# Routing stage of a two-layer mixture-of-experts backbone: expert matrices requested at the end of the output products, the prompt tile's stores on ScalarE's queue, two matrices behind the gathers, the affinities turned inside the last product

## The reference, cut to what matters

```python
def ec_moe(x, router_w, w_gate, w_up, w_down):
    bsz, n_tok, _ = x.shape
    cap = n_tok * EC_CAPACITY // N_EXPERTS
    aff = jax.nn.softmax(jnp.einsum('btd,de->bte', x, router_w).astype(jnp.float32), axis=-1)
    gate, idx = lax.top_k(jnp.swapaxes(aff, 1, 2), cap)
    bidx = jnp.arange(bsz)[:, None, None]
    xe = x[bidx, idx]
    hid = jax.nn.silu(jnp.einsum('becd,edf->becf', xe, w_gate)) * jnp.einsum('becd,edf->becf', xe, w_up)
    ye = jnp.einsum('becf,efd->becd', hid, w_down) * gate[..., None].astype(x.dtype)
    return jnp.zeros_like(x).at[bidx, idx].add(ye)
```

## Time and profile before

| What | us |
|---|---|
| three runs | 1542.63, 1538.18, 1542.36 |
| median | 1542.36 |
| profiled execution, its own time | 1539.78 |
| its span, first to last instruction | 1538.0 |
| TensorE busy in the span | 1337.5 (87%) |
| DMA engines, mean rate over the span | 220 GB/s |

### The profile page before, as it was taken

One profiled execution on the slowest core, in us unless ns is written; L12 is line 12 of the kernel. 1 busy time (PEld: TensorE's weight loads), 2 busy tenths in 40 slices (PEclk: granted clock), 3 DMA queues, 4 the chain that ended last, 5 costly groups with the idle time before them and its releaser, 6 DMA issues. The chain is left out here.

```text
span 1538.0 us, 17799 instructions
## 1 busy us (share of the span) xinstructions
PE 1337.5 (87%) x6717; PEld 933.7 (61%) x6717; DVE 1007.3 (65%) x1355; ACT 805.0 (52%) x1126; POOL 438.0 (28%) x264
## 2 busy tenths in 40 slices
PE   5989999677792999999989999988697499999995
PEld 1756567454681666666658877555376366666663
DVE  1536415765646888888866338566554688888875
ACT  3612116533422777777755277544322377777772
POOL 0002007554002044444330032355101024444430
PEclk7999999798995999999989999999798599999997
DMA  9578840300517999999951120040231999999954
GB/s 366 224 287 315 325 156 8 150 29 28 218 72 275 348 360 382 381 381 379 368 159 19 59 59 5 8 198 1 92 151 60 372 343 383 380 376 376 379 179 170
DMA packets 63598, 339.11 MB, mean 220 GB/s; under 512 B 16724, under 2 KB 21464, under 8 KB 45080
## 3 DMA queue, kind: packets, MB, share of 16 engines
q1 hardware_dynamic: 57464, 317.31, 54.1%
q0 software_dynamic: 6048, 20.65, 5.7%
HBM read 314.04 MB, written 23.89 MB: 220 GB/s over the span
## 5 line engine op out<-in xcount | busy, mean ns | idle before, releaser
L1696 POOL TENSOR_TENSOR modrow<-modrow,proj 80x1024 f32<-80x1024 f32 x30 | 132.6, 4420 | 311.2 <-ACT modrow L1814 311.2
L1846 DVE TENSOR_TENSOR wlow<-wraw,proj_rounded 128x2048 fp32r<-128x2048 f32 x96 | 217.0, 2288 | 5.3 <-ACT proj_rounded L1788 5.3
L1725 PE MATMUL psum<-wlow,proj_rounded 128*80 128x512 f32 x512 | 202.7, 396 | 0.0
L1788 ACT ACTIVATE proj_rounded<-wraw 128x2048 fp32r<-128x2048 f32 x96 | 180.0, 1909 | 9.2 <-PEq L1377 9.2
L1724 PE MATMUL psum<-proj_rounded 128*80 128x512 f32 x376 | 151.3, 402 | 2.1 <-DVE proj_rounded L1851 2.1
L1726 PE MATMUL psum<-proj_rounded 128*80 128x512 f32 x376 | 148.2, 394 | 0.0
L1304 POOL TENSOR_SCALAR ring<-ring,small 128x640 f32<-128x640 f32 x64 | 99.7, 1563 | 109.1 <-DVE small L1261 108.6
L1287 ACT ACTIVATE ring<-psum,small 128x640 f32<-128x640 f32 (+1 forms) x80 | 56.7, 709 | 100.1 <-DVE small L1255 100.1
L1846 DVE TENSOR_TENSOR wlow<-wraw,xr_rounded 128x2048 fp32r<-128x2048 f32 x32 | 73.3, 2291 | 43.7 <-ACT xr_rounded L1788 43.7
L1725 PEld LDWEIGHTS psum<-wlow,proj_rounded 128*80 128x80 f32 x512 | 76.8, 150 | 39.8 <-issue 1.2
L1725 PE MATMUL psum<-wlow,small_rounded 128*80 128x512 f32 x256 | 100.8, 394 | 0.0
(11 more groups left out here) (469 smaller groups left out, 3251.2 us busy)
## 6 DMA issues: line engine op xcount, KB each, us to landing
wraw<-in_exp_w_gate_dram SPq DMA_DIRECT2D x32, 2048.0 KB, 13.2
wraw<-in_exp_w_up_dram SPq DMA_DIRECT2D x32, 2048.0 KB, 12.6
wraw<-in_exp_w_down_dram SPq DMA_DIRECT2D x32, 2048.0 KB, 13.9
ring<-in_ada_w_dram SPq DMA_DIRECT2D x29, 1024.0 KB, 6.5
hold<-in_ada_w_dram SPq DMA_DIRECT2D x14, 1024.0 KB, 6.4
ring<-in_ev_w_in_dram SPq DMA_DIRECT2D x4, 2048.0 KB, 11.9
xr<-x_rows SPq DMA_DIRECT2D x15, 512.0 KB, 6.9
ring<-in_od_w_in_dram SPq DMA_DIRECT2D x3, 2048.0 KB, 17.0
```

Source lines behind the costliest of these rows:

```text
L1696: pool.tensor_tensor(ye[0:CAP, :], ye[0:CAP, :], g2[0:CAP, :], ALU.mult).then_inc(s["ye"], 1)
L1725: pe.matmul(dst, xs[:, 0, k, :], wl, start=False, stop=False)
L1788: act.activation(high_of(m, h), raw_of(m, h), ACT.Copy).then_inc(s["high"], 1)
L1846: dve.tensor_tensor(low_of(m, h), raw_of(m, h), high_of(m, h), ALU.subtract).then_inc(s["low"], 1)
```

## The change

In the out block SyncE stores only the four sample tiles. It then waits for the ten half products and requests matrices 2 to 5. The prompt tile's two stores are issued by ScalarE: x behind the root, xm behind a wait for the normalised tile, both ahead of the prompt tile's turned copy. The last half product is cut after two of its eight k steps, and the sample's affinities are turned there. VectorE takes four rounds of the sample ahead of the prompt tile's scaling and four behind it. In the experts block SyncE waits for gathers 0 and 1 to land before it requests matrices 6 and 7, and all that stands behind them in its queue waits too.

```diff
-                    for t in range(TILES):
+                    for t in range(ST):
                         sp.wait_ge(s["x"], 2 * (t + 1))
                         sp.dma_start(x_rows[t * P:(t + 1) * P, :], xr[:, t, :]).then_inc(s["st"], 16)
                         sp.wait_ge(s["xm"], t + 1)
                         sp.dma_start(xm_rows[t * P:(t + 1) * P, :], xm[:, t % 2, :]).then_inc(s[f"row{t % 2}"], 16)
-                        if t == PT:
-                            sp.wait_ge(s["mm"], 2 * TILES)
-                            for m in range(2, 6):
-                                load_weights(sp, l, m, ready)
-                    sp.wait_ge(s["st"], 16 * TILES)
-                    sp.wait_ge(s["row0"], 16 * 3)
+                    sp.wait_ge(s["mm"], 2 * TILES)
+                    for m in range(2, 6):
+                        load_weights(sp, l, m, ready)
+                    sp.wait_ge(s["st"], 16 * ST)
+                    sp.wait_ge(s["row0"], 16 * 2)
                     sp.wait_ge(s["row1"], 16 * 2)
+                    sp.wait_ge(s["stp"], 16)
+                    sp.wait_ge(s["rowp"], 16)
...
-                    product(PT, 1)
+                    product(PT, 1, 0, 2)
                     turn_affinities(0)
+                    product(PT, 1, 2, KD)
...
-                    choose(0, 0, 2)
+                    choose(0, 0, 4)
...
-                    choose(0, 2, ROUNDS[0])
+                    choose(0, 4, ROUNDS[0])
...
                     root(PT)
+                    act.dma_start(x_rows[PT * P:(PT + 1) * P, :], xr[:, PT, :]).then_inc(s["stp"], 16)
+                    act.wait_ge(s["xm"], TILES)
+                    act.dma_start(xm_rows[PT * P:(PT + 1) * P, :], xm[:, PT % 2, :]).then_inc(s["rowp"], 16)
                     turn_copy(PT)
...
                 def _(sp):
+                    for n in range(2):
+                        sp.wait_ge(s[f"gat{n}"], 16)
                     for m in range(6, NSLOT):
                         load_weights(sp, l, m, ready)
```

More of the change, by code:

```diff
@@ L1359, in out_and_route @@
             s = {n: sem(f"o{l}_{n}") for n in ("mods", "mm", "gx", "x", "sq", "root", "own", "xm", "turned", "copied",
-                                              "lg", "mx", "ex", "pt", "pown", "recip", "aff", "affT", "top", "it", "st", "row0", "row1",
+                                              "lg", "mx", "ex", "pt", "pown", "recip", "aff", "affT", "top", "it", "st", "row0", "row1", "stp", "rowp",
                                               "whigh", "wlow", "xhigh", "xlow")}
@@ L1392, in _, with product @@
                         sp.dma_start(xm_rows[t * P:(t + 1) * P, :], xm[:, t % 2, :]).then_inc(s[f"row{t % 2}"], 16)
-                        if t == PT:
-                            sp.wait_ge(s["mm"], 2 * TILES)
-                            for m in range(2, 6):
-                                load_weights(sp, l, m, ready)
-                    sp.wait_ge(s["st"], 16 * TILES)
-                    sp.wait_ge(s["row0"], 16 * 3)
+                    sp.wait_ge(s["mm"], 2 * TILES)
[3 more added lines that the diff above has]
+                    sp.wait_ge(s["row0"], 16 * 2)
                     sp.wait_ge(s["row1"], 16 * 2)
+                    sp.wait_ge(s["stp"], 16)
+                    sp.wait_ge(s["rowp"], 16)
                 @block.tensor
                 def _(pe):
-                    def product(t, h):
+                    def product(t, h, lo=0, hi=KD):
                         u = 2 * t + h
-                        if u >= 4:
+                        if lo == 0 and u >= 4:
                             pe.wait_ge(s["gx"], u - 3)
-                        if h == 0:
+                        if lo == 0 and h == 0:
                             pe.wait_ge(s["xlow"], t + 1)
-                        for k in range(KD):
+                        for k in range(lo, hi):
                             if u == 0 and k % 2 == 0:
@@ L1416, in product @@
                             mm = pe.matmul(bank(u % 4), x_low, wv_high[:, k, cut], start=False, stop=(k == KD - 1))
-                        mm.then_inc(s["mm"], 1)
+                        if hi == KD:
+                            mm.then_inc(s["mm"], 1)
                     def turn(t):
```

## The result

The changed kernel takes 1521.13 us (median of four runs, 1517.88 to 1521.77) beside 1540.33 for the kernel before (four runs). The ratio is 0.9874 with a 95% interval of 0.9852 to 0.9896, that is 16.0 to 22.8 us less. The forecast was 1528. Five more runs of the changed kernel beside the kernel before gave 0.9877 (0.9854 to 0.9900). The profiled execution took 1521.77 us with a span of 1520.0.

The account below looks back on a forecast made before the run. TensorE's wait for gather 0, behind the chain from affinities to indices, bounds the routing stage's end. Layer gains 6.9 + 6.0 = 12.9 us take 1539.8 to 1526.9, with the median's 2.6 1529.5; forecast 1528, range 1521 to 1536.

Parts of the forecast that it names:

- Early turn: Routing stage: turning the affinities inside the last half product starts the prompt's softmax 3.0 us earlier, at about 480.7.
- The stores: Routing block's end: the last prompt store lands at 487.6 and holds the block, leaving 1.3 us a layer instead of 3.0.
- The low end: Prompt tile's stores: with the store's own packet time of 0.138 us, the last one lands at 485.8.
- The bound of 489: Prompt tile's stores: if they get nothing until matrices 2 to 5 are through, they land at 488, at most 489.
- The gather: Gather 0 on near-empty queues takes 4.7 us, gaining 5.6 in layer 0 and 4.7 in layer 1.
- The floor: VectorE's first weight rests: a gather landing faster than about 4.3 us behind its issue brings nothing.
- Matrices 6 and 7: Expert stage: requested at about 495 instead of 488.94, they have 20 us of cover and cost nothing.
- B: Routing block's end: computation binds, stores land before 485.9, full 3.0 us had; time 1523 to 1527, chance 0.25.
- C: Gather 0: slow by itself, falling only to 8 us; time 1534, chance 0.12.
- D: Expert stage: the DMA engines set its length, gain 2.5 us a layer; time 1536, chance 0.06.
- E: Routing block's end: stores crawl and land at 502, each layer loses about 7 us; time 1555, chance 0.04.
- F: Routing block's end: stores land at 492 to 495, eating the gather's gain; time 1538 to 1545, chance 0.06.

Follow-up runs that it names:

- hold_only: Kernel before with only the wait of matrices 6 and 7 for gathers 0 and 1 added; ratio 1.0007.
- no_turn: Changed kernel with the affinity turn put back behind the whole last half product and the rounds back to 2 and 6; ratio 0.9912.
- turn_only: Kernel before with only the early affinity turn and the four-and-four rounds added; ratio 0.9960.
- turn_hold: Changed kernel with requests and stores as before the change, the early turn and the wait of matrices 6 and 7 kept; ratio 0.9963.
- sp_stores: Changed kernel with the prompt tile's two stores put on SyncE's queue behind the four matrix requests; ratio 0.9957.
- half_hold: Changed kernel with matrix 6 requested at the experts block's start and only matrix 7 held for the gathers; ratio 0.9956.
- hold_long: Changed kernel with matrices 6 and 7 held until the first expert product has ended; ratio 0.9885.

## Why the prediction fell short

The direction and the mechanism were right: a shorter chain to the indices, and a gather that no longer shares the DMA engines. The sum, 12.9, was 3.3 too low, of which 2.4 is the block's end (1.7 + 3.3 against 1.3 + 1.3) and 0.9 the gather. The medians have 3.0 more outside the stages, and together that is the way from the forecast to 1521.

- **Early turn.** Forecast 3.0 us to the prompt's softmax, computed from full-clock rows, and that term was right. At the full clock the softmax starts 24.6 us behind the affinities without the early turn (before and hold_only in layer 0, no_turn) and 21.4 with it (turn_only, turn_hold and sp_stores in layer 0, half_hold in layer 1): 3.2. Where both are caught by the low clock it is 3.4 (layer 1, 26.17 to 22.73). In layer 0 the profiles show only 1.9 (24.59 to 22.66), since there the changed kernel alone is caught: its matmuls take 0.63 us until 459.8, the 1.2 GHz level, where the kernel before has 0.40, the 2.4 GHz level.
- **The stores: the step that failed.** I let the stores, and not the computation, end the block: 487.6 for the last landing, 28.4 us behind the affinities, and so 1.3 us a layer. The xm store lands 27.6 behind them in both layers of the changed kernel, caught by the low clock, and 26.0 at the full clock, in half_hold's layer 1 (issued at 1188.92, 11.0 us, affinities at 1173.86). The block's end is then VectorE's to within half a microsecond, and gather 0 is issued 3.2 us earlier at the full clock (half_hold's layer 1 at 27.32, before at 30.56) and 3.3 in layer 1, where both kernels are caught. So the term is 3.2 a layer and not 1.3. That layer 0 shows only 1.7 is the clock again, and it is luck that the sum came as near as it did. Two things were mis-sized. I priced a store's packet like a gather's, 0.229 us, when the store's own row gave 0.138; measured beside the matrices it is 0.088 x 16 x 29 / 288 = 0.142. And I let ScalarE's queue wait for the root to end, but the store was issued at 469.16, ahead of the Sqrt at 470.43. The queue waits for the sum of squares, read by 469.12, and goes on once the Sqrt is handed over. The low end that I had worked out, 485.8, was the value to take; in this trace's time that is 485.0 against 486.0 measured, with the low clock.
- **The bound of 489 for stores behind all four matrices** did not hold: sp_stores has its last store at 492.8, in a trace whose affinities are 1.5 us later, so 491.3. The matrices' own packets are near the sum (71.1% of 29 us in the row above, 20.6 us of each engine, against 19.7). What I had not counted is the end: in sp_stores the DMA engines are only 0.07 and 0.02 busy in the last two microseconds before the landing, so a few packets of a few engines hold it. It cost the forecast nothing, but it made the expectation of sp_stores miss.
- **The gather.** 4.7 forecast, 4.09 and 4.30 measured, so 6.2 and 5.1 gained instead of 5.6 and 4.7. The floor was right: VectorE ends the first weight rests at 492.91 and goes on to the gathered rows at once. The last of matrices 2 to 5 landed at 489.9, behind gather 0's issue at 487.24, but its packets were all but through when the gather's first one moved at 489.0.
- **Matrices 6 and 7** cost nothing, as forecast, even held 6 us longer.
- **The rivals.** B came nearest: computation ends the block, level with the store, and its condition, a landing before 485.9, which is 26.7 behind the affinities, is met at the full clock. Its reason of a store that passes in one turn is not: the store's packets and the matrices' go one for one. C fell with the gather at 4.1, D with hold_long, E and F with the store's landing at 486.0. By the Trainium skill (DMA: Bandwidth & Descriptors, "Queues, rings and completion order") a completion waits for every earlier write of its DMA engine, across queues, and I had read that as putting the stores' end at the drain of the matrices. The xm store landed at 486.0 and the last of matrices 2 to 5 at 466.0 + 23.9 = 489.9, so it did not wait for what merely stood in the other queue.
- **Outside the stages.** 18.0 us between the two spans less 16.2 leaves 1.8: 0.8 ahead of layer 0's affinities, 0.5 between the two stages and 0.5 behind them. The medians leave 3.0. I had no term for it. The stretch with another clock accounts for 2.3 us, but it begins 1.5 us later in the changed kernel's profile, so only 0.8 is left of it. What the rest is stays open, and it is within the noise of the timings.

## What to carry over

A short transfer on the critical path wanted the DMA queues empty on both sides here: what was asked for before it has to be through when its first packet moves, and what comes next has to wait until it has landed. Each half alone gave nothing. Look for the next prefetch that is needed late, and put its request behind the landing of what is needed now. Where two chains end a block together, shortening one is not enough. And compare two profiles of a stage only where the granted clock is the same.

## What the runs showed of the hardware

- A gather of 80 rows of 4 KB takes 4.0 to 4.7 us with no matrix load beside it and 9.4 to 10.5 us beside matrix loads, whether one matrix or six are outstanding.
- Beside a busy queue the first packet of another queue moves 4.0 to 4.4 us behind a gather's issue and 3.4 to 3.8 us behind a store's, where a gather without that traffic has 1.6 to 1.8. From then on the two queues move as many packets each (109 and 111, 81 and 80), whatever their size.
- A 512 KB store on ScalarE's queue beside 8 MB on SyncE's lands in 10.1 to 12.5 us, on SyncE's own queue behind them in 16.7 to 22.6, alone in 2.6.
- ScalarE issued a store while its own table load of 1.28 us was under way, 1.3 us ahead of the Sqrt that stands before it in the program.
- A stretch of 99 us without a changed instruction took 96.8 to 99.1 us, with a granted clock of 0.93 to 0.90.
- Where the granted clock is 0.50 to 0.64 in the 2 us behind the affinities, the way from there to the gather is 1.1 to 1.6 us longer than where it is 1.00.
